# Expert weights in 2 MB transfers with 16 KB per partition, an eighth ring slot and four operand buffers

## The chip, the cores and the metric

One Trainium2 chip, one of its cores. The metric is the device time of one execution in microseconds, lower is better. The profile is one execution as the hardware profiler recorded it.

## What is computed

Three blocks in a row on 256 tokens of width 1024, all in fp32. The first is an attention and spatial-gating layer with a mixture of 16 experts, the second a macaron pair of half FFNs around an mLSTM mixer, the third an attention and an LRU layer. The change is in the experts of the first block:

```python
def expert_choice_ffn(h, w_router, w1, w3, w2):
    n, d = h.shape[1], h.shape[2]
    cap = CAPACITY_FACTOR * n // N_EXPERTS          # 32 tokens
    aff = jax.nn.softmax((h @ w_router).astype(jnp.float32), axis=-1)
    gate, idx = lax.top_k(jnp.swapaxes(aff, 1, 2), cap)
    xe = jax.vmap(lambda hb, ib: hb[ib])(h, idx)
    hid = jax.nn.silu(jnp.einsum('becd,edf->becf', xe, w1)) * jnp.einsum('becd,edf->becf', xe, w3)
    ye = jnp.einsum('becf,efd->becd', hid, w2) * gate[..., None].astype(h.dtype)
```

Each of the 16 experts has w1 and w3 of 1024 x 2048 and w2 of 2048 x 1024, 8 MB each in fp32: 384 MB in all, each byte read once and used for 32 tokens.

## The kernel before

Five programs, one for each engine, are written out by hand, in order, and meet through semaphores. Each engine has one semaphore on which it counts its instructions; `at(name)` is the count at which a named step is done. All loads of weights are issued by SP.

**The ring.** Weights go through `ring`, `NSLOT` = 7 slots of 1 MB (2048 fp32 in each of 128 partitions). `Ring.place` (L96) gives each load the next slot in turn, and passes over slots that are held. `load` (L220) has SP wait until the former owner of the slot is released, `("free", name)`, and issues the DMA. SP works strictly in order, so a load whose slot is not free holds up all that follow. `sp_experts` (L1681) issues for each expert x eight loads `(w1,x,kk)` of 128 rows, eight `(w3,x,kk)`, and eight `(w2,x,c,hf)` of 256 rows, each 1 MB with 8 KB in one run per partition. A slot `gs` is held during expert 0 for the scatter weights, with no load.

**The experts on TensorE.** `pe_experts` (L1715) waits for each load and multiplies it with the gathered tokens: w1 and w3 at L1775, w2 at L1799, four products side by side on 32 columns each. The last product that reads a slot releases it. Between w3 and w2 stands the turn of the expert: VectorE multiplies (L1945), TensorE transposes `sil` (L1789), VectorE copies the result (L1947, `hid`), and w2 begins. After w2 VectorE scales `ye` (L1956), and TensorE scatters it during the next expert (L1759).

**The second block's units.** A part of the second block is woven into the experts as 44 units, from expert 2 on, one in about 7.5 of the 24 places of an expert (`unit_at`). Unit u brings one load, a chunk `(s,12+u)` of 1 MB, mostly with 1 KB rows; two units bring none, and after unit 34 the number is one less. ScalarE (L323) and VectorE (L329) split a chunk into a high and a low part in `WB`; the end of VectorE's split releases the slot. On VectorE the units stand at fixed places in the order: those of the w1 places at the beginning of the expert, those of the w3 places before its product, those of the w2 places after `hid`. TensorE multiplies the chunk a unit later (L231 to L233).

**The operands.** The down projections (`pe_rows`, L457) of the later blocks use activations that ScalarE (`act_operand`, L492) and VectorE (`dve_operand`, L499) split into `RB`, two buffers; operand n waits until TensorE has finished with operand n-2. `pe_rows` holds back operand nk-2 and works off the last two together.

Of the kernel before, what the change touches and what calls it, by code (L numbers as in the profile page):

```python
# [11 lines left out]
D = 1024  # L12
NSLOT = 7
BIG = 12626
# [70 lines left out]
class Ring:  # L85
# [7 lines left out]
    def clear(self):  # L93
        self.i, self.owner, self.count, self.held = 0, [None] * NSLOT, [0] * NSLOT, {}

    def place(self, name, hold, loads):  # L96
        while self.i % NSLOT in self.held.values():
            self.i += 1
        i = self.i % NSLOT
        self.i += 1  # L100
        before, self.owner[i] = self.owner[i], name
        self.count[i] += 16 * loads
        self.slot[name], self.value[name], self.before[name] = i, self.count[i], before
        if hold:
            self.held[name] = i
        return i, before

# [34 lines left out]
def _build(nc, I, out, ctx):  # L142
# [10 lines left out]
    WB = sb("WB", [128, 2, 2, 2048], F32R)  # L153
    RB = sb("RB", [128, 2, 2, 512], F32R)
    big = sb("big", [128, BIG])
# [64 lines left out]
    def load(sp, name, src, n, pat=None, hold=False, parts=128, **dims):  # L220
        i, before = R.place(name, hold, 1)
        if before is not None:
            sp.wait_ge(*at("free", before))
        sp.dma_start(slot(name, n, pat, parts, **dims), src).then_inc(R.sem[i], 16)

    def free_before(name):
# [10 lines left out]

    def rows2(w, c0=0, n=D):  # L240
# [58 lines left out]
    def load_chunk(sp, c):  # L299
        src, n, pat, dims = CH[c]  # L300
        if not isinstance(src, tuple):
            load(sp, ("s", c), src, n, pat, **dims)
            return
        i, before = R.place(("s", c), False, 2)
        sp.wait_ge(*at("free", before))
        for q in range(2):
            sp.dma_start(slot(("s", c), n, pat, **dims)[:, q], src[q]).then_inc(R.sem[i], 16)
# [80 lines left out]

    def pe_turning(pe, name, tiles, regions, xn, waits=(), ends=(), b0=0):
        for w in waits:  # L390
            pe.wait_ge(*at(*w))
        for kk in range(8):
            b = b0 + kk % 4
            if kk >= 4:
                pe.wait_ge(*at("turned", name, kk - 4, 0))
                if len(regions) == 2:
                    pe.wait_ge(*at("turned", name, kk - 4, 1))
            for i, (ap, n, r, c) in enumerate(tiles):
                z = 0 if c < regions[0][1] else 1
                if kk == 0:  # L400
                    pe.wait_ge(*at("xn", name, i))
                closes = i + 1 == len(tiles) or (z == 0 and len(regions) == 2 and tiles[i + 1][3] >= regions[0][1])
                e = pe.transpose(PB[4 * z + b][:, c:c + n], xn(i)[0:n, kk * 128:kk * 128 + 128], ident[0:n, 0:n])
# [116 lines left out]

    def act_row(act, name, dst, bank):
        for z in range(2):
            yield
            act.wait_ge(*at("row", name, z))
            act.activation(dst[:, 512 * z:512 * z + 512], PB[bank][:, :], ACT.Copy).then_inc(*A(("rowed", name, z)))

# [216 lines left out]
    def pe_gemv(pe, group, waits):  # L743
        def pick(v):
            pe.wait_ge(*at("mraw", v))
            raw, rows_ = gemv_raw(v), ident.rearrange("p (j c) -> p j c", j=4)[:, :, 0:2]
            for i in range(4):
                if v == TWO:
                    for a in range(2):
                        e = pe.matmul(gemv_bank(v)[:, 8 * i:8 * i + 4].rearrange("p (j c) -> p j c", c=2), raw[:, 128 * i:128 * i + 128],  # L750
                                      rows_[:, 2 * a:2 * a + 2], start=a == 0, stop=a == 1)
                else:
                    e = pe.matmul(gemv_bank(v)[:, 8 * i:8 * i + 8].rearrange("p (j c) -> p j c", c=2), raw[:, 128 * i:128 * i + 128],
                                  rows_, start=True, stop=True)
            e.then_inc(*P(("pick", v)))
# [303 lines left out]
    def act_first(act):  # L1059
# [54 lines left out]
        for n in range(4):  # L1114
            steps(g2, 2)
        run(act_row(act, "gt", gt1, 5))

# [563 lines left out]
    def sp_experts(sp, g2):  # L1681
        steps(g2, 8)
        load(sp, "router", I["w_router"][0].rearrange("(a p) n -> p a n", p=128), 128, "p (a n) -> p a n", a=8)
        run(g2)
# [30 lines left out]
    def pe_experts(pe, g2):  # L1715
# [9 lines left out]
        steps(g2, 8)  # L1725
        pe_turn(pe, "h2", TL2, REG_2, lambda i: xn_2[:, i, :], between=route)
        pe.wait_ge(*at("aff"))
# [10 lines left out]
        for kk in range(8):  # L1738
# [3 lines left out]
            for i in range(2):  # L1742
                pe.matmul(PB[b][:, :], xh[:, i, kk * 128:kk * 128 + 128], posr[:, i, :], start=i == 0, stop=False)
                e = pe.matmul(PB[b][:, :], xl[:, i, kk * 128:kk * 128 + 128], posr[:, i, :], start=False, stop=i == 1)
            e.then_inc(*P(("gathered", kk)))
# [20 lines left out]
        for x in range(16):  # L1766
            for half, name in ((0, "w1"), (1, "w3")):
                if x:
                    pe.wait_ge(*at("ye", x - 1, half))
                for kk in range(8):  # L1770
                    steps(ctx_units, len(units(x, 8 * half + kk)))
                    s = slot((name, x, kk))
                    pe.wait_ge(*landed((name, x, kk)))
                    for j in range(4):
                        e = pe.matmul(PB[half][32 * j:32 * j + 32, :], xeT[:, kk, 32 * x:32 * x + 32], s[:, 512 * j:512 * j + 512],  # L1775
                                      start=kk == 0, stop=kk == 7)
                    e.then_inc(*P(("free", (name, x, kk)), *([("up", x, half)] if kk == 7 else [])))
                    if x and half == 0 and kk % 2:
# [8 lines left out]
            for j in range(4):  # L1787
                c0 = 256 * (j // 2) + j % 2
                e = pe.transpose(PB[0][:, 128 * j:128 * j + 128], sil[:, c0:c0 + 255:2], ident)  # L1789
            e.then_inc(*P(("hid_turned", x)))  # L1790
            pe.wait_ge(*at("hid", x))
            for c in range(4):
                steps(ctx_units, len(units(x, 16 + 2 * c, 2)))
                for n in range(2):
                    for j in range(4):
                        if n == 0 and j % 2 == 0:
                            pe.wait_ge(*landed(("w2", x, c, j // 2)))
                        s = slot(("w2", x, c, j // 2), 2048, "p (j n) -> p j n", j=2)
                        e = pe.matmul(PB[n][32 * j:32 * j + 32, :], hidT[:, j, 32 * c:32 * c + 32],  # L1799
                                      s[:, j % 2, 512 * n:512 * n + 512], start=c == 0, stop=c == 3)  # L1800
                        if n == 1 and j % 2:
                            e.then_inc(*P(("free", ("w2", x, c, j // 2)), *([("down", x)] if c == 3 and j == 3 else [])))
            if x == 1:
# [5 lines left out]
    def act_experts(act, sp_, g2):  # L1809
# [24 lines left out]
        for x in range(16):  # L1834
# [8 lines left out]
            if x == 0:  # L1843
                scatter_weights(1)
                run(act_row(act, "gt2", gt2, 4))
            steps(ctx_units, len(units(x, 16, 8)))
# [1778 lines left out]
def layout(I):  # L3625

    def c(v):
        v = np.asarray(v).reshape(-1)
        return v.reshape(-1, 128).T
    b_in = np.asarray(I["b_in_2"])[0]  # L3630
# [4 lines left out]
    parts = {"c": c(I["c"]), "c_ctx": c(I["c_ctx"]), "b_mod": c(I["b_mod"]), "g_mix": c(I["g_mix"]),  # L3635
             "g_ffn": c(I["g_ffn"]), "c_2": c(I["c_2"]), "c_ctx_2": c(I["c_ctx_2"]), "b_ada_2": c(I["b_ada_2"]),
             "norm_g_2": c(I["norm_g_2"]), "b_q": c(b_in[512:1536]), "b_k": c(b_in[1536:2560]),
# [34 lines left out]
```

## Time and profile before

| | before |
|---|---|
| time, median of 3 runs | 2356.17 us (2351.1 to 2356.51) |
| span of the profiled execution | 2347.7 us |
| TensorE busy (matmul) | 1993.4 us, 85% |
| VectorE / ScalarE busy | 962.5 us, 41% / 734.3 us, 31% |
| moved by DMA | 672.10 MB, mean 286 GB/s |
| mean granted TensorE clock | 0.935 of 2.4 GHz |

The span runs from the first to the last instruction; the time of an execution also has what lies around it, 8.5 us more in the median. The page's slices are 58.7 us each. The experts stand from 270 to 1350 us, the first block's attention before them, the second and third blocks after them.

### The profile page before, as it was taken

How to read it: one execution, taken by the hardware profiler on the slowest of the kernel's cores; microseconds unless marked ns; L12 is line 12 of the kernel's file. 1: busy time of each engine (PE TensorE's matmuls, PEld its weight loads, DVE VectorE, ACT ScalarE, POOL GpSimd, SP SyncE). 2: the span in 40 equal slices, each digit the busy share in tenths (PEclk: the TensorE clock that was granted, in tenths of full speed). 3: DMA queues.
4: the chain of work that ended last, by engine and by line, in shares of the span. 5: the costliest groups of instructions: out<-in, count | busy, mean ns of one | idle time of the engine just before them, and what ended most of it. 6: DMA issues, size and time to landing. Idle time of an engine off the chain costs nothing.

```text
span 2347.7 us, 29615 instructions
## 1 busy us (share of the span) xinstructions
PE 1993.4 (85%) x12486; PEld 1349.9 (57%) x12486; DVE 962.5 (41%) x1623; ACT 734.3 (31%) x1190; POOL 42.6 (2%) x47
## 2 busy tenths in 40 slices
PE   6999767778777777777778789989999899999997
PEld 3656313333334333333434389968999899785686
DVE  3534321122122122212434254567664645653486
ACT  4322221011111111112211054454654544543365
POOL 0000000000000000000000000000000000000010
PEclk8989899898999899898889999999999999999999
DMA  9967899999999999999999965535444455350430
GB/s 371 418 244 273 330 409 418 413 413 414 414 417 411 412 414 416 413 410 406 410 396 413 412 209 183 173 112 161 126 142 164 162 171 187 110 186 19 144 131 23
DMA packets 210436, 672.10 MB, mean 286 GB/s; under 512 B 11504, under 2 KB 134512, under 8 KB 152192
## 3 DMA queue, kind: packets, MB, share of 16 engines
q1 hardware_dynamic: 210304, 670.21, 74.3%
q8 instruction: 99, 1.62, 0.3%
q14 instruction: 33, 0.27, 0.0%
HBM read 669.12 MB, written 1.05 MB: 285 GB/s over the span
## 4 chain that ended last, share of the span: by engine, by line
PE 54%; DMA 30%; DVE 11%; ACT 3%; issue 2%; SPq 0%; POOL 0%; DVEq 0%; ACTq 0%
DMA ring<-in_w 22%; PE pb L231 12%; PE pb L233 12%; PE pb L232 12%; DMA ring<-in_w_a 5%; PE pb L1775 3%; DVE WB L329 3%; PE pb L1799 2%; DMA ring<-in_w_in 2%; PE pb L770 2%; ACT WB L323 1%; DMA ring<-in_w_mod 1%; PE pb L994 1%; PE pb L964 1%; PE pb L3053 1%
## 5 line engine op out<-in xcount | busy, mean ns | idle before, releaser
L329 DVE TENSOR_TENSOR WB<-ring,WB 128x1024 fp32r<-128x1024 f32 (+3 forms) x370 | 426.4, 1194 | 454.1 <-ACT WB L323 453.4
L323 ACT ACTIVATE WB<-ring 128x1024 fp32r<-128x1024 f32 (+3 forms) x370 | 361.3, 1025 | 725.9 <-DMA ring<-in_w_a 456.8
L231 PE MATMUL pb<-HH,WB 128*128 128x256 f32 (+1 forms) x1680 | 494.1, 294 | 11.1 <-DVE WB L329 4.3
L232 PE MATMUL pb<-HL,WB 128*128 128x256 f32 (+1 forms) x1680 | 483.6, 288 | 0.0
L233 PE MATMUL pb<-HH,WB 128*128 128x256 f32 (+1 forms) x1680 | 483.3, 288 | 0.0
L1775 PE MATMUL pb<-ring,big 128*32 128x512 f32 x2048 | 296.3, 671 | 149.5 <-DMA ring<-in_w 132.5
L231 PEld LDWEIGHTS pb<-HH,WB 128*128 128x128 f32 x1680 | 330.4, 197 | 38.3 <-issue 23.2
L232 PEld LDWEIGHTS pb<-HL,WB 128*128 128x128 f32 x1680 | 330.5, 197 | 2.2 <-issue 2.1
L233 PEld LDWEIGHTS pb<-HH,WB 128*128 128x128 f32 x1680 | 329.9, 196 | 0.0
L1775 PEld LDWEIGHTS pb<-ring,big 128*32 128x32 f32 x2048 | 47.4, 113 | 362.1 <-DMA ring<-in_w 274.8
L1799 PE MATMUL pb<-ring,big 128*32 128x512 f32 x1024 | 166.6, 644 | 55.5 <-DMA ring<-in_w 46.9
L231 PE MATMUL pb<-WB,RB 128*128 128x512 f32 x376 | 154.1, 410 | 11.8 <-DVE RB L501 11.0
L232 PE MATMUL pb<-WB,RB 128*128 128x512 f32 x376 | 150.4, 400 | 0.0
L233 PE MATMUL pb<-WB,RB 128*128 128x512 f32 x376 | 150.0, 399 | 0.0
L1799 PEld LDWEIGHTS pb<-ring,big 128*32 128x32 f32 x1024 | 35.5, 113 | 164.6 <-DMA ring<-in_w 99.5
L231 PE MATMUL pb<-WB,HH 128*128 128x256 f32 (+2 forms) x368 | 120.9, 328 | 7.8 <-DVE big L2750 2.8
L233 PE MATMUL pb<-WB,HL 128*128 128x256 f32 (+2 forms) x368 | 118.2, 321 | 0.0
L232 PE MATMUL pb<-WB,HH 128*128 128x256 f32 (+2 forms) x368 | 118.0, 321 | 0.0
L1926 DVE TENSOR_TENSOR X<-X,pb 128x512 f32<-128x512 f32 x64 | 44.0, 687 | 163.7 <-PE pb L1759 163.5
L231 PEld LDWEIGHTS pb<-WB,RB 128*128 128x128 f32 x376 | 73.1, 194 | 39.3 <-DVE RB L501 14.0
L1759 PE MATMUL pb<-big 128*128 128x512 f32 x128 | 72.9, 656 | 17.0 <-DVE X L1926 16.2
L770 PE MATMUL pb<-ring,cs 128*32 128x512 f32 x480 | 66.7, 681 | 20.0 <-DMA ring<-in_w_mod 18.1
(450 smaller groups left out, 1955.3 us busy)
## 6 DMA issues: line engine op xcount, KB each, us to landing
ring<-in_w SPq DMA_DIRECT2D x384, 1024.0 KB, 14.3
ring<-in_w_a SPq DMA_DIRECT2D x66, 1024.0 KB, 11.8
ring<-in_w_in SPq DMA_DIRECT2D x38, 1024.0 KB, 7.0
ring<-in_w_ada SPq DMA_DIRECT2D x36, 1024.0 KB, 6.6
ring<-in_w_b SPq DMA_DIRECT2D x33, 1024.0 KB, 5.0
ring<-in_w_mod SPq DMA_DIRECT2D x24, 1024.0 KB, 11.1
ring<-in_w_out SPq DMA_DIRECT2D x8, 1024.0 KB, 6.1
ring<-in_b_w_in SPq DMA_DIRECT2D x8, 1024.0 KB, 6.5
```

The costliest lines, as they stand in the source:

```text
L231: pe.matmul(o, l[0], r[0], start=start, stop=False)
L232: pe.matmul(o, l[0], r[1], start=False, stop=False)
L233: return pe.matmul(o, l[1], r[0], start=False, stop=stop)
L323: act.activation(WB[:, c % 2, 0, x:y], flat[:, x:y], ACT.Copy).then_inc(*A(("high", c, z)))
L329: dve.tensor_tensor(WB[:, c % 2, 1, x:y], flat[:, x:y], WB[:, c % 2, 0, x:y].bitcast(F32), ALU.subtract).then_inc(*V(("low", c, z), *([("f ...
L770: e = pe.matmul(gemv_bank(v)[32 * j:32 * j + 32, :], cs_flat[:, 16 * which + 2 * kk:16 * which + 2 * kk + 32], s[:, 512 * j:512 * j + 512] ...
L964: pe.matmul(PB[3 + n % 3][:, :], qT1[r:r + 64, pl, 128 * i:128 * i + 128], kT1[r:r + 64, :], start=True, stop=True).then_inc(*P(("scores1" ...
L994: e = pe.matmul(PB[2 * (h % 2) + z][:, 256 * s_:256 * s_ + 256], kT1[r:r + 64, c:c + 128], qT1[r:r + 64, pl, :], start=True, stop=True)
L1759: pe.matmul(PB[moe_bank(x, i, j)][:, :], gT[:, x, 128 * i:128 * i + 128], ye[:, 512 * j:512 * j + 512], start=True, stop=True).then_inc(*P ...
L1775: e = pe.matmul(PB[half][32 * j:32 * j + 32, :], xeT[:, kk, 32 * x:32 * x + 32], s[:, 512 * j:512 * j + 512], start=kk == 0, stop=kk == 7)
L1799: e = pe.matmul(PB[n][32 * j:32 * j + 32, :], hidT[:, j, 32 * c:32 * c + 32], s[:, j % 2, 512 * n:512 * n + 512], start=c == 0, stop=c == 3)
L1926: dve.tensor_tensor(y, y, PB[moe_bank(x, i, j)][:, :], ALU.add).then_inc(*V(("moe", x, i, j)))
```

## The change

- `ring` has 8 slots. Each expert matrix is loaded in four transfers of 2 MB, each into two neighbouring slots (`place_pair`), with 16 KB in one run per partition: `(w1,x,q)`, `(w3,x,q)` with q = 0 to 3, `(w2,x,c)` with c = 0 to 3. A transfer is released when both its halves have been used.
- `place_pair` takes the pointer's slot and the next. Where the next is beyond slot 7 or one of the two is held, it puts the slot into a list `left` (if it isn't itself held) and moves on. `place` for a single load that is not held takes the last entry of `left` first.
- A pair of rows of w1 lies in one partition, so the model width is used in another column order (`by_pairs`) by the transposes of `xn_2`, the gather of the tokens, the columns of modulation, bias and gain, and the router. `act_row` brings two gate rows back into the usual order. w2 has four rows in a partition, so `sil` is transposed in steps of four columns.
- The loads of the units stand ahead of the pair whose places they share.
- `RB` has four buffers; operand n waits for operand n-4.
- The scratch space of the DMA rings is reduced, which makes room.

The core of the diff:

```diff
-NSLOT = 7
+NSLOT = 8
+    def take(self, i, n, name, loads):
+        before = [x for x in dict.fromkeys(self.owner[i:i + n]) if x is not None]
+        self.owner[i:i + n] = [name] * n
+        self.count[i] += 16 * loads
+        self.slot[name], self.value[name] = i, self.count[i]
+        self.before[name] = before[0] if before else None
+        return i, before
+
     def place(self, name, hold, loads):
+        if self.left and not hold:
+            return self.take(self.left.pop(), 1, name, loads)
         while self.i % NSLOT in self.held.values():
             self.i += 1
         i = self.i % NSLOT
         self.i += 1
...
+    def place_pair(self, name):
+        while True:
+            i = self.i % NSLOT
+            held = [j for j in (i, i + 1) if j in self.held.values()]
+            if i + 1 < NSLOT and not held:
+                break
+            if i not in held:
+                self.left.append(i)
+            self.i += 1
+        self.i += 2
+        return self.take(i, 2, name, 1)
...
+    def load_pair(sp, name, src):
+        i, before = R.place_pair(name)
+        for b in before:
+            sp.wait_ge(*at("free", b))
+        sp.dma_start(pair(name), src).then_inc(R.sem[i], 16)
...
+    def by_pairs(kk):
+        c = 256 * (kk // 2) + kk % 2
+        return slice(c, c + 255, 2)
...
     def rb(n, w):
-        return RB[:, n % 2, 0, 0:w], RB[:, n % 2, 1, 0:w]
+        return RB[:, n % 4, 0, 0:w], RB[:, n % 4, 1, 0:w]
...
-        if n >= 2:
-            act.wait_ge(*at("operand", name, n - 2))
+        if n >= 4:
+            act.wait_ge(*at("operand", name, n - 4))
...
             for name, w_ in (("w1", w1), ("w3", w3)):
-                for kk in range(8):
-                    for u in units(x, 8 * (name == "w3") + kk):
+                for q in range(4):
+                    for u in units(x, 8 * (name == "w3") + 2 * q, 2):
                         load_unit(u)
-                    load(sp, (name, x, kk), w_[x, kk * 128:kk * 128 + 128, :], 2048)
+                    load_pair(sp, (name, x, q), w_[x, 256 * q:256 * q + 256, :].rearrange("(p b) n -> p (b n)", b=2))
...
             for c in range(4):
-                for hf in range(2):
-                    for u in units(x, 16 + 2 * c + hf):
-                        load_unit(u)
-                    load(sp, ("w2", x, c, hf), w2[x, 512 * c + 256 * hf:512 * c + 256 * hf + 256, :].rearrange("(p b) n -> p (b n)", b=2), 2048)
+                for u in units(x, 16 + 2 * c, 2):
+                    load_unit(u)
+                load_pair(sp, ("w2", x, c), w2[x, 512 * c:512 * c + 512, :].rearrange("(p b) n -> p (b n)", b=4))
...
                 for kk in range(8):
                     steps(ctx_units, len(units(x, 8 * half + kk)))
-                    s = slot((name, x, kk))
-                    pe.wait_ge(*landed((name, x, kk)))
+                    s = pair((name, x, kk // 2))
+                    if kk % 2 == 0:
+                        pe.wait_ge(*landed((name, x, kk // 2)))
...
-                e = pe.transpose(PB[0][:, 128 * j:128 * j + 128], sil[:, c0:c0 + 255:2], ident)
+                e = pe.transpose(PB[0][:, 128 * j:128 * j + 128], sil[:, j:j + 509:4], ident)
```

## Rows read from the trace of the kernel before

**Rows 1.** The page, part 2: tenths in 40 slices of 58.7 us.

```profile
PE   6999767778777777777778789989999899999997
...
DMA  9967899999999999999999965535444455350430
GB/s 371 418 244 273 330 409 418 413 413 414 414 417 411 412 414 416 413 410 406 410 396 413 412 209 183 173 112 161 126 142 164 162 171 187 110 186 19 144 131 23
```

**Rows 2.** Busy time by stretch: us, engines busy, clock, DMA share, GB/s.

```profile
core 0: us, PE busy (x) PEld busy (x) DVE busy (x) ACT busy (x) POOL busy (x), PEclk, DMA share, GB/s
308.00:368.00 60.00, 39.73 (x225) 8.49 (x219) 13.85 (x27) 8.20 (x16) 0.00 (x0) 0.91 1.01 421
270.00:1346.00 1076.00, 828.31 (x5132) 376.35 (x5124) 265.74 (x408) 150.50 (x210) 4.96 (x4) 0.91 1.01 411
1408.00:1467.00 59.00, 59.00 (x494) 59.00 (x493) 29.04 (x34) 24.27 (x31) 0.00 (x0) 1.00 0.57 186
```

**Rows 3.** The chain of waits, 270 to 1346 us, shares by line.

```profile
by line: DMA ring<-in_w 47.2%; DMA ring<-in_w_a 11.2%; PE pb L1775 7.1%; PE pb L1799 5.0%; PE pb L231 4.8%; PE pb L232 4.4%; PE pb L233 4.4%; DMA ring<-in_w_in 3.9%; DVE WB L329 2.8%; ACT WB L323 1.3%; PE pb L1759 1.3%; issue 0.7%; DVE tmpT
```

**Rows 4.** Loads issued from L224, 308 to 368 us.

```profile
L224 SPq DMA_DIRECT2D ring<-in_w x26: 327/328/679, 308.2 to 367.5; - x26
...
DMA to landing us min/median/max: 12.5/15.4/16.2
```

**Rows 5.** The same, 127 to 170 us, where the queue runs empty.

```profile
L224 SPq DMA_DIRECT2D ring<-in_w_ada x10: 327/328/328, 127.2 to 169.3; - x10
...
DMA to landing us min/median/max: 4.8/5.3/6.7
```

**Rows 6.** Timeline of expert 6: start, duration, what, idle before; w3, turn, chunk.

```profile
700.43 1.94 PE L1775 MATMUL pb<-ring,big 128*32 128x512 f32 x8 [1.42 <-DMA ring<-in_w]
...
702.92 1.94 PE L1775 MATMUL pb<-ring,big 128*32 128x512 f32 x8 [0.55 <-DMA ring<-in_w]
...
705.41 1.70 PE L1775 MATMUL pb<-ring,big 128*32 128x512 f32 x8 [0.55 <-DMA ring<-in_w]
707.19 0.69 DVE L1945 TENSOR_TENSOR big<-big,pb 128x512 f32<-128x512 f32 x1 [13.26 <-PE pb L1775]
...
708.71 0.69 DVE L1947 COPY big<-pb 128x512 f32<-128x512 f32 x1 [0.84 <-PE pb L1789]
710.89 2.00 ACT L323 ACTIVATE WB<-ring 128x1024 fp32r<-128x1024 f32 x2 [18.41 <-DMA ring<-in_w_a]
```

**Rows 7.** Timeline at the start of expert 0.

```profile
270.64 38.59 SPq L224 DMA_DIRECT2D ring<-in_w  x19
...
276.23 1.06 PE L1775 MATMUL pb<-ring,big 128*32 128x512 f32 x8 [1.34 <-DMA ring<-in_w]
```

**Rows 8.** Timeline, the split of a chunk in expert 8.

```profile
863.56 2.01 ACT L323 ACTIVATE WB<-ring 128x1024 fp32r<-128x1024 f32 x2 [16.87 <-DMA ring<-in_w_a]
...
864.65 2.36 DVE L329 TENSOR_TENSOR WB<-ring,WB 128x1024 fp32r<-128x1024 f32 x2 [14.46 <-ACT WB L323]
```

**Rows 9.** Timeline at the last operand of the first half FFN.

```profile
1547.45 0.42 ACT L497 ACTIVATE RB<-big 128x256 fp32r<-128x256 f32 x1 [2.30 <-PE pb L233]
...
1547.90 0.43 DVE L501 TENSOR_TENSOR RB<-big,RB 128x256 fp32r<-128x256 f32 x1 [1.79 <-ACT RB L497]
...
1548.47 0.47 PE L231 MATMUL pb<-WB,RB 128*128 128x512 f32 x1 [1.12 <-DVE RB L501]
```

**Rows 10.** TensorE's waits, 1350 to 2348 us: total, times, longest.

```profile
PE pb L231 <- DVE RB L501: 11.0, 8, 3.2
```

**Rows 11.** Groups of instructions by line: busy, mean ns, idle before.

```profile
L582 PEld LDWEIGHTS pb<-K,big 128*128 128x128 f32 x80 | 14.7, 212 | 25.8 <-DVE big L623 25.8
...
L1789 PEld LDWEIGHTS pb<-K,big 128*128 128x128 f32 x64 | 9.6, 209 | 34.8 <-DVE big L1945 34.5 <-issue 0.2
...
L525 ACT ACTIVATE big<-pb 128x512 f32<-128x512 f32 x6 | 3.6, 597 | 11.2 <-PE pb L519 11.2
```

More of the change, by code:

```diff
@@ L100, in place @@
         self.i += 1
-        before, self.owner[i] = self.owner[i], name
-        self.count[i] += 16 * loads
-        self.slot[name], self.value[name], self.before[name] = i, self.count[i], before
         if hold:
             self.held[name] = i
-        return i, before
+        return self.take(i, 1, name, loads)
+    def place_pair(self, name):
[9 more added lines that the diff above has]
+        return self.take(i, 2, name, 1)
     def let_go(self, name):
@@ L221, in load, with pair @@
         i, before = R.place(name, hold, 1)
-        if before is not None:
-            sp.wait_ge(*at("free", before))
+        for b in before:
+            sp.wait_ge(*at("free", b))
         sp.dma_start(slot(name, n, pat, parts, **dims), src).then_inc(R.sem[i], 16)
+    def pair(name):
+        i = R.slot.get(name, 0)
+        return ring[:, i:i + 2, :].rearrange("p s n -> p (s n)")
+    def load_pair(sp, name, src):
+        i, before = R.place_pair(name)
+        for b in before:
+            sp.wait_ge(*at("free", b))
+        sp.dma_start(pair(name), src).then_inc(R.sem[i], 16)
     def free_before(name):
@@ L304, in load_chunk @@
         i, before = R.place(("s", c), False, 2)
-        sp.wait_ge(*at("free", before))
+        for b in before:
+            sp.wait_ge(*at("free", b))
         for q in range(2):
@@ L384, in act_scaled, with pe_turning @@
                 act.activation(xn(i)[0:n, :], ap, ACT.Copy, scale=st[0:n, r:r + 1]).then_inc(*A(("xn", name, i)))
-    def pe_turning(pe, name, tiles, regions, xn, waits=(), ends=(), b0=0):
+    def pe_turning(pe, name, tiles, regions, xn, waits=(), ends=(), b0=0, block=by_blocks):
         for w in waits:
@@ L1115, in act_first @@
             steps(g2, 2)
-        run(act_row(act, "gt", gt1, 5))
+        run(act_row(act, "gt", gt1, 5, True))
         for q in (0, 2):
@@ L1682, in sp_experts @@
         steps(g2, 8)
-        load(sp, "router", I["w_router"][0].rearrange("(a p) n -> p a n", p=128), 128, "p (a n) -> p a n", a=8)
+        load(sp, "router", I["w_router"][0].rearrange("(q p b) n -> p q (b n)", q=4, b=2), 128, "p (q n) -> p q n", q=4)
         run(g2)
@@ L1725, in pe_experts @@
         steps(g2, 8)
-        pe_turn(pe, "h2", TL2, REG_2, lambda i: xn_2[:, i, :], between=route)
+        pe_turn(pe, "h2", TL2, REG_2, lambda i: xn_2[:, i, :], between=route, block=by_pairs)
         pe.wait_ge(*at("aff"))
@@ L1795, in pe_experts @@
                     for j in range(4):
-                        if n == 0 and j % 2 == 0:
-                            pe.wait_ge(*landed(("w2", x, c, j // 2)))
-                        s = slot(("w2", x, c, j // 2), 2048, "p (j n) -> p j n", j=2)
+                        if n + j == 0:
+                            pe.wait_ge(*landed(("w2", x, c)))
+                        s = pair(("w2", x, c)).rearrange("p (j n) -> p j n", j=4)
                         e = pe.matmul(PB[n][32 * j:32 * j + 32, :], hidT[:, j, 32 * c:32 * c + 32],
-                                      s[:, j % 2, 512 * n:512 * n + 512], start=c == 0, stop=c == 3)
-                        if n == 1 and j % 2:
-                            e.then_inc(*P(("free", ("w2", x, c, j // 2)), *([("down", x)] if c == 3 and j == 3 else [])))
+                                      s[:, j, 512 * n:512 * n + 512], start=c == 0, stop=c == 3)
+                e.then_inc(*P(("free", ("w2", x, c)), *([("down", x)] if c == 3 else [])))
             if x == 1:
@@ L1844, in act_experts @@
                 scatter_weights(1)
-                run(act_row(act, "gt2", gt2, 4))
+                run(act_row(act, "gt2", gt2, 4, True))
             steps(ctx_units, len(units(x, 16, 8)))
```

39 lines of the change are left out of this document (24 added, 15 removed).

## The prediction

> **What bounds the kernel now.** I read the page's forty slices first: from slice 6 to slice 23 the DMA row stands at 9, GB/s at 390 to 418, while TensorE stands at 6 to 8 [rows 1]. The table by stretch gives the same stage in one row: 270 to 1346 us, 1076 us, the 16 DMA engines at a share of 1.01 and 411 GB/s, TensorE busy 828 us [rows 2]. The chain of waits over that stretch is 62% DMA into `ring` (47.2 + 11.2 + 3.9) [rows 3]. So in 46% of the span the DMA queue is the bound, and a microsecond in which it has nothing to move is a microsecond of the kernel. What keeps it full is depth: a 1 MB load there lands 12.5 to 16.2 us after its issue [rows 4], the time of some six loads, while a load into an empty queue needs 4.8 [rows 5]. After 1350 us DMA is at about half (0.57) and TensorE has no gap in a whole slice [rows 2]: there the change can act only through the operand buffers.
>
> Two prices follow. Successive expert loads let TensorE start at 700.43, 702.92 and 705.41: 2.49 us for 1 MB [rows 6]. So an empty queue costs 4.8 - 2.49 = 2.3 us between an issue and full flow. Call it the restart.
>
> **Part 1, longer runs.** The cost of a packet by its length: at 1 KB rows 186 GB/s at share 0.57 is 326 GB/s for busy engines, 50.2 ns for each 1,024-byte packet on one of 16; at 8 KB rows 421 at 1.01 is 417, 314.4 ns [rows 2]. The slope is 264.2 / 7168 = 0.0369 ns a byte, the constant 12.5 ns. A 16 KB packet is then 616.5 ns instead of 628.8, 2.0%. The 1 KB rows come from a queue with pauses, which inflates their price, so I take 1.7%, with 0 (long rows are cut again) and 3% as bounds. The 192 pairs cost 2 x 2.49 = 4.98 us each now; 192 x 4.98 x 0.017 = 16 us saved (0 to 28). The Trainium skill, page "DMA: Bandwidth & Descriptors", section "Bandwidth", gives a fixed 3 cycles a packet, 3.5 ns at its 850 MHz, where the rows give 12.5; by it, as an estimate, the gain would be 5 us. Its ceiling of 435 GB/s would leave 3% above the 421 of the trace.
>
> **Part 2, where the loads go.** This part decides. I walked `Ring.place` and `place_pair` through the load order of `sp_experts` and noted for each load whose release SP awaits and how many MB were issued behind that one. Before: always 6 (5 while `gs` is held). After: mostly 7 or 5, but not always, because of `left`. `place_pair` puts a slot that it skips into `left`, the pointer laps and a later pair takes that slot in the ordinary way, yet it stays in `left`, and the next chunk of the second block takes it, whoever has it by then. Three kinds result.
>
> (a) A chunk is put into the slot of the pair issued just before: `(s,30)` behind `(w1,7,3)`, `(s,46)` behind `(w3,12,3)`, `(s,48)` behind `(w1,13,2)`. SP waits until that pair has landed and been multiplied; nothing is queued behind. TensorE takes 1.06 us for 1 MB [rows 7], 2.1 for a pair (3.9 at the lower clock of [rows 6], 1.94 each). Idle: 2.1 + 2.3 = 4.4 us, three times, 13.2.
>
> (b) A pair needs slots 6 and 7 just after a chunk went to 7: `(w1,6,1)` behind `(s,26)`, `(w1,11,1)` behind `(s,42)`. SP waits for the split of the chunk. ScalarE starts at 863.56, VectorE ends at 864.65 + 2.36 = 867.01: 3.45 us [rows 8]. Idle: 3.45 + 2.3 = 5.75, twice, 11.5.
>
> (c) The same at the turn of an expert: `(w2,6,0)` behind `(s,28)`, `(w2,11,0)` behind `(s,44)`. The split stands on VectorE behind `hid`, which needs the last w3. From that landing: 2.1 for TensorE, then 2.3 from the end of its matmuls (707.11) to the end of the copy (709.40), then 2.36 of VectorE; 6.8. The chunk lands 3.0 after w3 (710.89 - 705.41 - 2.49) [rows 6, 8]. Idle: 6.8 - 3.0 + 2.3 = 6.1, twice, 12.2.
>
> (d) Seven pairs wait for a chunk with one pair (4.9 us) between: `(w1,2,1)`, `(w3,2,1)`, `(w2,4,3)`, `(w3,5,2)`, `(w2,9,3)`, `(w3,10,2)`, `(w1,15,3)`. Idle: 5.75 - 4.9 = 0.9 each, 6.
>
> (e) In expert 0 `gs` has slot 3, slot 2 can't be paired, and only three pairs circulate, 6 MB as before but released two at a time. Before, SP resumes at 270.64, 1.1 us after TensorE's start [rows 7]; then 2.1. With the pauses for the scatter weights, where the released pair again comes late: 3 us (1 to 5).
>
> (f) 54 pairs cover halves of two former pairs and have 5 MB behind the later one, 12.4 us. A pair takes 2.1, a unit of the second block on TensorE between them about 6, a turn 2.3, the restart 2.3: 12.7. So it is about even where a unit and a turn meet, and short where the heavier units of experts 10 to 14 stand. No row prices that; bounds 0 and 20 us, I take 6, near the lower end since few of the 44 units meet a turn.
>
> Sum of idle: 13.2 + 11.5 + 12.2 + 6 + 3 + 6 = 52 us. All of it falls on the bound; nothing later in the stage can win it back, since the share is 1.01 [rows 2].
>
> **Part 3, four operand buffers.** `act_operand` of the last operand waits for the last but two; `pe_rows` holds its last two operands back, so TensorE meets an unready operand at the end of each down projection: ScalarE 1547.45, VectorE 1547.90, TensorE 1548.47 after 1.12 us idle [rows 9]. Of the 11.0 us in eight waits [rows 10] five are of this kind, in fa, wo2, fb, wo3 and wob; 5 x 1.12 = 5.6 us go (4 to 6). The other three wait for VectorE's states and stay. Next after it is the split of the chunk, which has landed and been split earlier.
>
> **Part 4, the rest.** The eighth slot before 270 us: the queue is full there only from about 60 to 120 us, by rate [rows 1]; elsewhere TensorE and VectorE set the pace. 1 us gained (0 to 3). Strided reads of the weights for transposes: the `sil` transposes already read every second column, at 209 ns a weight load against 212 for unstrided ones [rows 11]; stride 4 isn't shown, 64 loads, bounds 0 and +0.2 us each, 13 at most but under the waits for DMA, so 0. Six copies with interleaved columns, 0.6 us each [rows 11], up to twice that; 0 (to 3). The router's load has half as many pieces and lands before it is needed; 0. After the last load TensorE works 2 us as before; 0.
>
> **The sum.** -16 + 52 - 5.6 - 1 = +29.4 us. The profiled span is 2347.7; the median of the three runs is 2356.2, 8.5 more, which I leave as it is: 2377 for a span, **2386** for the time.
>
> **The rivals.** *Free transfers (faster).* The releases come early enough or the waits of (a) to (c) lie where the queue has slack; then 2356 - 16 - 5.6 - 1 = 2333. For it: TensorE idles a quarter of the stage. Against it: the share of 1.01, and in (a) to (c) nothing is queued at all. It decides if the idle adds up to less than 16 us. 0.10. *Even.* Idle between 16 and 30 us, 2356. 0.06. *Cascade.* In (f) every one of the 44 units leaves the ring 1.5 us short: 66 instead of 6, 2446. For it: 12.4 against 12.7 above. Against it: most units stand away from turns. 0.09. *Rows cut again.* The 16 KB runs move in packets as before, part 1 is 0: 2402. 0.10. *A fixed price per transfer.* If each transfer paid its restart in a full queue, 192 fewer would save 192 x 2.3 = 442 us, 1914. The 2.49 us between successive starts [rows 6] against 4.8 [rows 5] speak against that. 0.01. The fit in the same page of the Trainium skill, section "Anatomy of one DMA", has such a fixed 2.0 us per DMA and its rule is to batch; the trace shows it hidden in a full queue. *The forecast* has 0.64.
>
> **Range.** Low: (a) to (c) 37, (d) to (f) 6, gain 22 + 7: +14, 2370; a little below it to take in part of the even case, 2367. High: (f) 20, lower clock in (a) and (c) 9 more, gain 8: 37 + 9 + 6 + 3 + 20 - 8 - 5 = +62, cut to 2414, since they hardly all meet. The measurement tells 0.3%, 7 us, from no change. Faster: free transfers and the fixed price, 0.11. Same: 0.06. Slower: forecast, cascade and cut rows, 0.83.
>
> **What would show it.** Right: GB/s near 428 where several pairs run in a row; holes of 4 to 6 us in the DMA row at seven places of the stage, with SP waiting for TensorE's or VectorE's release; no waits of 1.12 us at the ends of the down projections; the stage ending some 36 us later. Wrong: a share of 1.01 through the stage (then the free transfers hold), or idle of a microsecond or two at every unit (cascade). The prediction fails most easily on (f) and on the 1.7%.

## The result, and the profile after

| | before | after |
|---|---|---|
| time, median | 2354.22 us (2351.1 to 2356.51) | 2439.45 us (2438.82 to 2440.01) |
| span of the profiled execution | 2347.7 us | 2438.6 us |
| mean granted TensorE clock | 0.935 | 0.909 |

The change makes the kernel slower: ratio 1.0371, 95% interval 1.0354 to 1.0387, 85 us. The forecast was 2386 us, 2367 to 2414. The sign was right, the size was not. (The median of before now has a fourth run in it.)

The page of after, part 2, the last two rows as in [rows 1]; a slice is 61.0 us:

```profile
DMA  9967798999997999998979995534517445351330
GB/s 385 414 241 290 304 417 356 421 386 378 403 370 306 423 394 392 389 371 358 379 310 373 370 379 185 179 108 163 159 62 233 157 158 188 122 179 52 123 128 18
```

The flat 410 to 418 GB/s of [rows 1] has gone. Two slices, 421 and 423, are above everything that before shows; next to them stand 356, 306 and 310. The long runs are faster, and the queue is stopped more. The stretches of after, in the columns of [rows 2]:

```profile
270.00:1440.00 1170.00, 834.67 (x5133) 397.83 (x5136) 266.26 (x411) 150.33 (x210) 4.96 (x4) 0.86 0.93 378
...
540.00:730.00 190.00, 137.12 (x840) 66.38 (x840) 36.64 (x45) 21.19 (x27) 0.00 (x0) 0.88 0.94 386
```

The expert stage ends at 1440 us, not at 1346; its DMA share is 0.93 for 1.01. TensorE is busy 834.7 us in it, for 828.3: its work is nearly the same, it waits more. The chain of waits of the stage begins, in the form of [rows 3]:

```profile
by line: DMA ring<-in_w 51.5%; PE pb L1816 10.1%; DMA ring<-in_w_a 7.8%; PE pb L260 4.1%; PE pb L1840 3.9%; PE pb L261 3.7%; PE pb L262 3.6%; DVE WB L366 2.7%; DMA ring<-in_w_in 1.9%; PE pb L1798 1.2%; PE pb L1522 1.1%; issue 1.0%; SPq L253
```

L1816, the product with w1 and w3 (L1775 of before), has risen from 7.1% to 10.1% of a longer stretch: where the queue is empty, the chain goes from a transfer to the products that read it, to their release, and to the next transfer.

**The queue's time, load by load.** For each load of the stage I took the distance between its landing and the one before, and subtracted what the load takes in a full queue: 2.487 us for 1 MB in 8 KB runs, 4.898 us for a pair in 16 KB runs, 2.5 to 2.97 us for a chunk. What is left is called idle time of the queue. In every kernel it also holds about 4 us in which the queue isn't idle but moves two loads that don't go to the ring, `b_v` ahead of `(s,48)` (1.4 us) and `ctx_2` ahead of `(w2,3,0)` (2.5 us); they cancel in differences. The count begins behind the first 6 MB of the experts. The two kernels, and the twelve that follow, compare so. Idle and end of stage are from the profiled execution, whose own time can lie off the median of the runs: it was 2377.5 us in e1, 2352.7 in e3, 2354.5 in e4, 2346.8 in e12. Each ratio is against before on the same chip; before had medians of 2349 to 2353 us there:

| kernel | time, us | ratio to before, 95% | last w2 landed, us | idle of the queue, us |
|---|---|---|---|---|
| before | 2354.2 | | 1346.7 | 24.2 |
| after | 2439.5 | 1.0371 (1.0354 to 1.0387) | 1439.9 | 130.3 |
| e1_no_left | 2385.0 | 1.0138 (1.0114 to 1.0161) | 1379.5 | 72.9 |
| e2_short_runs | 2448.2 | 1.0402 (1.0381 to 1.0423) | 1444.3 | 124.0 |
| e3_rb4 | 2347.3 | 0.9971 (0.9958 to 0.9985) | 1351.3 | 26.1 |
| e4_8slots | 2349.6 | 0.9988 (0.9977 to 0.9998) | 1345.5 | 23.2 |
| e5_halves | 2357.7 | 1.0014 (1.0000 to 1.0029) | 1352.3 | 44.7 |
| e6_left_halves | 2418.8 | 1.0276 (1.0252 to 1.0301) | 1416.4 | 110.3 |
| e7_8slots_rb4 | 2343.6 | 0.9961 (0.9948 to 0.9974) | 1339.5 | 21.7 |
| e8_wrap | 2346.7 | 0.9960 (0.9945 to 0.9975) | 1344.5 | 33.2 |
| e9_wrap_units_first | 2333.2 | 0.9921 (0.9903 to 0.9939) | 1330.7 | 21.3 |
| e10_units_first | 2400.5 | 1.0214 (1.0195 to 1.0233) | 1397.3 | 88.8 |
| e11_no_left_first | 2346.8 | 0.9969 (0.9955 to 0.9983) | 1344.4 | 35.2 |
| e12_halves_first | 2340.7 | 0.9936 (0.9918 to 0.9954) | 1344.9 | 36.1 |

After against before: 14.3 us less for moving the bytes (1044.1 for 1058.4), 106.1 us more idle, the last w2 93.2 us later, and 2.4 us less for all that follows it. So the loss is idle time of the queue in the expert stage; the question is which waits make it.

**Who stops the queue.** SP's own waits in the stage of after, 270 to 1440 us: total, times, longest. A wait of SP is harmless while enough is queued behind it; these are only the candidates.

```profile
SPq L252 <- PE pb L1816: 205.5, 42, 17.5
SPq L252 <- DVE WB L366: 194.3, 17, 23.1
```

By kind of the prediction the idle of after is: (a) 6.8, 5.8, 4.6 at the three chunks, 17.2 (the third, `(s,48)`, lands 8.88 us behind the pair, but it takes 4.3 in the kernels where the queue does not stop there, 2.9 for itself and 1.4 for `b_v`); (b) 6.5 and 6.8, 13.2; (c) 9.4 and 8.5, 17.9; (d) 16.4 at seven pairs; (e) 1.8; and what remains above the 24.2 us of before, the kind (f), 39.6, most of it at pairs whose last release is 4 or 5 MB back. A replay of the placement gives 83 pairs with 5 MB and 21 with 4 MB behind the release that they await. Six of the 21 belong to expert 0; the other 15 wait for a slot that a chunk had, and lose 21 us, the 83 lose 23. Two of the stops of kind (f) are `(w3,13,3)` with 8.9 us and `(w3,14,1)` with 5.5.

One stop of kind (a) and one of kind (f), in the timeline of after (columns as in [rows 6]). First the chunk `(s,30)`, issued from L243:

```profile
788.19 1.92 PE L1816 MATMUL pb<-ring,big 128*32 128x512 f32 x16
...
790.18 0.38 SPq L243 DMA_DIRECT2D ring<-in_w_a  x1
```

The pair ahead of it was multiplied until 790.11, and 0.07 us later SP issues the chunk. Nothing is queued, as forecast. But the queue had run empty at 785.5 us already (the chunk lands at 795.3, 9.75 us behind the pair): TensorE, late from a unit two pairs before, took the landed pair up only at 788.19. Then `(w3,8,2)`, issued from L253:

```profile
864.07 1.93 PE L1816 MATMUL pb<-ring,big 128*32 128x512 f32 x8 [4.87 <-DMA ring<-in_w]
865.93 0.29 PEld L260 LDWEIGHTS pb<-WB,RB 128*128 128x128 f32 x1 [1.66 <-issue]
...
872.47 0.39 PE L262 MATMUL pb<-WB,RB 128*128 128x512 f32 x1
...
872.78 1.06 PE L1816 MATMUL pb<-ring,big 128*32 128x512 f32 x8
...
873.96 0.33 SPq L253 DMA_DIRECT2D ring<-in_w  x1
```

TensorE is idle for 4.87 us until `(w1,8,3)` has landed whole. Then it multiplies the first half, then works off a unit of the second block, 865.93 to 872.86, then multiplies the second half and releases. SP issues `(w3,8,2)` at 873.96; the queue's last transfer had landed at 873.79. This is the place where most of what I missed lies.

### The profile page after: what moved, and what is told of

Same layout as the page of the kernel before. It is cut to its first block, busy times and chain, and to the rows that moved or that the text cites. A ratio compares the mean times of both kernels' runs of the same rounds, so it can differ in the third digit from the quotient of the medians.

```text
span 2438.6 us, 29505 instructions
## 1 busy us (share of the span) xinstructions
PE 2002.8 (82%) x12486; PEld 1376.0 (56%) x12486; DVE 958.7 (39%) x1623; ACT 731.6 (30%) x1190; POOL 42.6 (2%) x47
## 4 chain that ended last, share of the span: by engine, by line
PE 53%; DMA 30%; DVE 10%; ACT 3%; issue 2%; SPq 1%; POOL 0%; DVEq 0%; ACTq 0%; POOLq 0%
DMA ring<-in_w 25%; PE pb L260 12%; PE pb L261 11%; PE pb L262 11%; PE pb L1816 5%; DMA ring<-in_w_a 4%; DVE WB L366 3%; PE pb L1840 2%; PE pb L810 2%; ACT WB L360 1%; DMA ring<-in_w_mod 1%; DMA ring<-in_w_in 1%; PE pb L1034 1%; PE pb L1798 1%; PE pb L1004 1%
## 5 line engine op out<-in xcount | busy, mean ns | idle before, releaser
L1816 PE MATMUL pb<-ring,big 128*32 128x512 f32 x2048 | 299.8, 710 | 202.1 <-DMA ring<-in_w 196.7
L260 PEld LDWEIGHTS pb<-HH,WB 128*128 128x128 f32 x1680 | 334.6, 199 | 43.7 <-issue 27.1
L262 PEld LDWEIGHTS pb<-HH,WB 128*128 128x128 f32 x1680 | 334.1, 199 | 0.0
L1816 PEld LDWEIGHTS pb<-ring,big 128*32 128x32 f32 x2048 | 60.2, 119 | 394.9 <-DMA ring<-in_w 217.6
L1840 PE MATMUL pb<-ring,big 128*32 128x512 f32 x1024 | 153.1, 730 | 85.2 <-DMA ring<-in_w 79.0
L1840 PEld LDWEIGHTS pb<-ring,big 128*32 128x32 f32 x1024 | 30.9, 121 | 179.6 <-DMA ring<-in_w 108.9
L260 PEld LDWEIGHTS pb<-WB,RB 128*128 128x128 f32 x376 | 73.8, 196 | 34.6 <-issue 11.5
## 6 DMA issues: line engine op xcount, KB each, us to landing
ring<-in_w SPq DMA_DIRECT2D x192, 2048.0 KB, 14.3
```

Source lines behind the costliest of these rows:

```text
L260: pe.matmul(o, l[0], r[0], start=start, stop=False)
L262: return pe.matmul(o, l[1], r[0], start=False, stop=stop)
```

## The experiments

**e1 to e4: one part each.** e1 leaves the list of skipped slots unused, so that every load goes on round the ring; a skipped slot is lost for that lap.

```diff
-            if i not in held:
-                self.left.append(i)
```

> The changed kernel with one edit: a slot that place_pair skips is not put into left, so single loads take the pointer's slot. By a replay of the placement every load then has at least 4 MB queued behind the load whose release it awaits; the seven distances of 0 and the seven of 2 are gone. Theory placement (stale entries of left make the loss): the seven holes with nothing queued (49.7 us in the trace of the changed kernel) and the seven with one pair queued (16.4 us) go, and so does most of the other 39 us, time 2335 to 2350. Rival coarse release (2 MB are released at once, and 5 MB behind are too few at a unit): only those 66 us go and some 40 remain, 2365 to 2385. Rival transfer size (2 MB transfers in themselves are slow): above 2420.

Measured 2385.0 us, 54.5 less than after and at the upper end of the rival of the coarse release. Kinds (a) to (d) are gone (0.8 us is left of them), and 49 us of idle above before are still there, so the stale slots are half of the loss and not its whole.

e2 gives each pair as two transfers of 1 MB, 8 KB in one run, same slots, waits and releases.

```diff
-        sp.dma_start(pair(name), src).then_inc(R.sem[i], 16)
+        for h in range(2):
+            sp.dma_start(pair(name)[:, 2048 * h:2048 * h + 2048], src[:, 2048 * h:2048 * h + 2048]).then_inc(R.sem[i], 16)
```

> The changed kernel with each 2 MB transfer issued as two of 1 MB with 8 KB runs, into the same slots, with the same waits and the same release. It isolates the length of the runs. By the prediction's part 1 and the 4.90 us between landings of successive pairs (twice 2.49 before) it costs 0.08 us a pair, 15 us: 2454. If long runs are worth nothing: 2439. If 2 MB transfers hurt: below 2435.

Measured 2448.2, 8.7 more than after, where 15 were expected: 13.8 us more for moving the bytes, 6.3 less idle. In moving, the long runs are worth what was forecast; in time, less. Whether they go out whole is also in the count of packets, part 3 of the page, first before, then after:

```profile
q1 hardware_dynamic: 210304, 670.21, 74.3%
```

```profile
q1 hardware_dynamic: 182144, 670.20, 71.0%
```

28,160 fewer packets for the same bytes. The 192 pairs halved from 256 to 128 packets are 24,576 of them. Another 3,072 are packets of 4 bytes, of which the traces show 16 for each transfer, and there are 192 transfers fewer; the last 512 are missing in e2 too, whose count is 209,792. Rows are not cut again.

e3 and e4 are before with four operand buffers, and before with eight slots.

```diff
-    RB = sb("RB", [128, 2, 2, 512], F32R)
+    RB = sb("RB", [128, 4, 2, 512], F32R)
...
-NSLOT = 7
+NSLOT = 8
```

> The kernel before with four operand buffers and nothing else. By part 3 of the prediction five waits of 1.12 us at the ends of the down projections go: 5.6 us faster than before, 2348.6. Rival: the wait moves to the split of the last chunk, 0 to 2 us.

> The kernel before with eight slots of 1 MB, and nothing else but the smaller scratch space. By part 4 of the prediction about 1 us faster (0 to 3), 2353. Rival: depth is short at the heavier units of experts 12 to 14 (landings 1 to 1.4 us late there) and at the start of expert 0, then 4 to 8 us faster.

e3: 0.9971, 6.8 us less than before on the same chip, 3.5 to 9.9 by the interval, and 4.7 by the medians (2347.3 and 2352.0). TensorE's waits behind the stage in e3, the row that answers to [rows 10] (11.0 us in eight waits):

```profile
PE pb L231 <- DVE RB L501: 6.5, 4, 3.4
```

After has 5.6 us in three waits there. The five waits of 1.12 us are gone or nearly so. e4: 0.9988, 2.8 us (0.5 to 5.4), 2.4 by the medians. Both small terms hold in time.

**e5 and e6: release by halves.** The products of a pair give back each 1 MB slot when they have read it; e5 does it on top of e1, e6 on after with its list.

```diff
-        self.owner[i:i + n] = [name] * n
+        self.owner[i:i + n] = [name] if n == 1 else [(name, 0), (name, 1)]
...
-                    if kk % 2:
-                        e.then_inc(*P(("free", (name, x, kk // 2)), *([("up", x, half)] if kk == 7 else [])))
+                    e.then_inc(*P(("free", ((name, x, kk // 2), kk % 2)), *([("up", x, half)] if kk == 7 else [])))
```

> The changed kernel with passed-over slots forgotten (as in e1_no_left) and, besides, each 1 MB half of a pair handed back by TensorE as soon as it has read that half (four matmuls earlier than the other half for w1 and w3). Counting the ring's order out, the last release that a load of the expert stage needs then lies at most 4 MB back in 6 pairs, 5 MB in 114, 6 MB in 71; in e1_no_left it is 30, 126 and 35; in the kernel before it is 6 MB nearly everywhere. THEORY (what is left over the kernel before is the release of 2 MB at once: the ring has less work queued behind it, and the loss sits in the loads with the shortest distance): most of e1's 49 us of extra idle goes, total 2345 to 2368 us. RIVAL A (the loss is the 2 MB transfer itself, the 2.9 us of restart in place of 2.3 us and a longer wait at each stop): 2375 to 2385 us, as e1_no_left. RIVAL B (the lower TensorE clock costs it): also near 2380 us, with the granted clock of the stage unchanged against e1_no_left.

> The changed kernel as it is, passed-over slots kept in its list, and each 1 MB half of a pair handed back separately. Last release at 4 MB or less: 23 pairs (32 in the changed kernel), at 5 MB 37 (83), at 6 MB or more 132 (77). THEORY (two causes that add: stale slots cost 54 us, coarse release some 20 to 40 us): 2400 to 2422 us, that is, the coarse release is worth about the same with the list as without it. RIVAL (the two losses overlap, since a stop for one refills the slack for the other): 2425 to 2439 us. If the list only hurt because the release was coarse: 2350 to 2370 us.

e5: 2357.7, 27.3 less than e1; e6: 2418.8, 20.7 less than after. By the ratios, which take before on the same chip, it is 29 and 22 us. Both lie where the theory put them, and the list costs 61 us with halves, 54.5 without: two causes that add. Rival B falls too: the granted clock of 270 to 1340 us is 0.87 in e5 and 0.88 in e1, with 27 us between them. But e5 left one stop of 12.2 us at `(w3,13,3)`, which halves could not shorten; e8 showed why.

**e7 and e8: is it the 2 MB, or the ring?** e7 is before with both small parts and nothing else. e8 is e5 with no slot ever skipped: a pair takes the next two slots, and where these are not neighbours (22 of 192) it goes as two transfers with a wait each.

```diff
+        a, b = ab
+        if b == a + 1:
+            i, before = self.take(a, 2, name, 1)
+            self.both[name] = None
+            return ab, before
```

> The kernel before with 1 MB transfers of 8 KB runs, plus only the eighth slot and the four operand buffers. THEORY (the two are separate: 5.6 us and 1 us forecast, 4.7 to 6.8 and 2.4 to 2.8 us measured alone): 2343 to 2348 us, ratio to before 0.995 to 0.998. RIVAL (both cover the same stops): 2346 to 2350 us.

> As e5_halves, but a pair takes the next two slots of the ring whatever they are: neighbours get one transfer of 2 MB in 16 KB runs, slots 7 and 0 (22 pairs of 192) get two transfers of 1 MB in 8 KB runs, each with its own wait. No slot is ever passed over. Last release at 5 MB: 5 pairs, at 6 MB or more all others, as in the kernel before. THEORY (distance to the last release sets the idle time): the extra idle over the kernel before falls to 0 to 8 us, the long runs keep 0.077 us on 170 pairs, 13 us, the operand buffers 5 us: 2332 to 2345 us, which beats both kernels. RIVAL (a 2 MB transfer stops the queue more whatever the distance): 2355 to 2375 us.

e7: 2343.6, as forecast, faster than before. e8: 2346.7, between theory and rival. Its last releases are as far back as in before, yet it has 9 us more idle, nearly all of it in one stop: 10.05 us at `(w3,13,3)`, where before lost 1.9 about that place (3.3 with `b_v`). Its timeline:

```profile
1156.37 1.93 PE L1844 MATMUL pb<-ring,big 128*32 128x512 f32 x8 [6.18 <-DMA ring<-in_w]
1158.23 0.58 PE L289 MATMUL pb<-WB,HH 128*128 128x256 f32 x1
...
1165.77 1.07 PE L1844 MATMUL pb<-ring,big 128*32 128x512 f32 x8
...
1176.83 2.05 PE L1827 MATMUL pb<-big 128*128 128x512 f32 x2 [9.99 <-DVE X L1994]
```

and VectorE's longest wait between 1150 and 1190 us:

```profile
DVE big L1739 <- PE pb L291: 11.0, 1, 11.0
```

TensorE waits 6.18 us for a whole pair, multiplies one half, and only then does the unit (1158.23 to 1165.8) for which VectorE has waited 11.0 us, with ten more microseconds of VectorE's work behind it, for which TensorE in turn waits 9.99. The same unit and the same wait in before:

```profile
1161.88 0.39 PE L231 MATMUL pb<-WB,HH 128*128 128x256 f32 x1
...
1178.93 2.05 PE L1759 MATMUL pb<-big 128*128 128x512 f32 x2 [10.05 <-DVE X L1926]
```

The wait of ten microseconds is thus not new (10.05 in before, 9.13 in e9 below). What differs is when the unit begins: in before at 1161.88, when the first of the two MB had landed at 1160.38 and been multiplied, and 5.3 us ahead of the second at 1167.13; in e8 1.9 us behind the whole pair. That is the stop of the timeline at 864 us again, with a longer tail.

**e9 and e10: the unit ahead of the pair's wait.** One edit in the order on TensorE: the units of both halves are worked off before the wait for the pair. Their chunks are loaded ahead of the pair already. e9 is e8 with it, e10 is after with it.

```diff
-                    steps(ctx_units, len(units(x, 8 * half + kk)))
+                    if kk % 2 == 0:
+                        steps(ctx_units, len(units(x, 8 * half + kk, 2)))
```

> As e8_wrap, with one edit in TensorE's order: a context unit that stands at the odd half of a w1 or w3 pair is computed ahead of the wait for that pair, not between its two halves (its chunk is already loaded ahead of the pair). The trace of e8_wrap has one large stop left that the kernel before has not: 10.05 us ahead of w3,13,3, where 3.3 us are lost in before. There TensorE waited 6.2 us for the whole pair w1,13,3, landed at 1156.33, then computed one unit of 7 us until 1165.8, for which VectorE waited 11.0 us with a 21 us chain behind it; in before the unit started when the first MB had landed, while the second was still on its way. THEORY (waiting for 2 MB at once delays the unit that stands between the halves): the stop ahead of w3,13,3 falls to 2 to 5 us, the total to 2336 to 2343 us, ratio to before 0.992 to 0.996. RIVAL (the stop comes from the chain on VectorE alone, and the order on TensorE only moves the wait): 2344 to 2348 us, and the stop stays at 8 us or more.

> The changed kernel with only that edit in TensorE's order: units at an odd half ahead of their pair's wait. Its stop ahead of w3,13,3 is 8.94 us. THEORY: 5 to 8 us less there, 2 to 4 us at the other 14 units that stand at an odd half, total 2427 to 2434 us. RIVAL (the stale slots' and the coarse release's stops swallow it): 2435 to 2440 us.

e10: 2400.5, 39 us less than after, three to seven times what I expected. e9: 2333.2, 0.9921 (0.9903 to 0.9939), a little below the range in time and within it by ratio; it beats before and after, and e7 too (0.9948 to 0.9974). The stop at `(w3,13,3)` is 0.6 us in e9. The place of the timeline above, now in e10:

```profile
846.76 1.15 PE L260 MATMUL pb<-WB,RB 128*128 128x512 f32 x1
...
852.76 0.39 PE L262 MATMUL pb<-WB,RB 128*128 128x512 f32 x1
...
853.08 1.92 PE L1817 MATMUL pb<-ring,big 128*32 128x512 f32 x16
...
855.11 0.33 SPq L253 DMA_DIRECT2D ring<-in_w  x1
```

The unit runs from 846.76 to 853.15 while `(w1,8,3)` is on its way (landed 850.89), both halves follow without a gap, and `(w3,8,2)` is issued at 855.11, with the landing of 860.66 still ahead of it: no stop. My expectation counted the 15 units that stand at an odd half and one pair for each. An explanation, which no run takes apart, is that TensorE, once late by a unit, releases every pair late until the next wait for data, so that one unit costs at more than one pair. In e10 the idle at pairs with a last release 4 or 5 MB back is 18.8 us, of which 10.2 is the start of expert 0; in after it is 54.7, with 10.4. The 15 pairs with 4 MB lose 0.9 us in e10 for 21 in after, with the same placement: 4 MB behind the release is enough once the unit stands ahead of the wait.

**e11 and e12: the ladder.** e11 is after with the edits of e1 and e10, e12 adds the halves of e5.

> The changed kernel with two edits: passed-over slots forgotten (e1_no_left, 54 us alone) and units at an odd half ahead of their pair's wait (e10_units_first, 39 us alone). Releases stay those of 2 MB. THEORY (the two stops lie at different loads: the stale slots at 11 pairs and 3 chunks, the late units at the 104 pairs whose last release is 4 or 5 MB back, which fell from 54.7 to 18.8 us in e10): nearly additive, 2344 to 2354 us. RIVAL (without the list 156 pairs instead of 104 have a last release 4 or 5 MB back, and the coarse release stops them whatever stands between the halves): 2356 to 2370 us.

> As e11_no_left_first, and each half of a pair handed back by itself (e5_halves with TensorE's units first). In e5_halves 27 us came from the separate halves. THEORY (the units between the halves were what used the slack up, so the coarse release costs little once they are gone): 3 to 10 us less than e11, 2337 to 2347 us. RIVAL (the coarse release costs the same 20 to 27 us as in e5 and e6): 20 to 27 us less than e11. Against e9_wrap_units_first (2333.2 us) it shows what 42 passed-over slots are worth: 4 to 12 us more than that.

e11: 2346.8. From after the two edits take 92.7 us, alone they took 39.0 and 54.5: they add. e12: 2340.7, 6.1 us less, within the theory; the two intervals just miss each other. The profiled spans are alike (2345.1 and 2345.4), but that of e12 is the slowest of its four runs. The coarse release, 20 to 27 us while units stood between the halves, costs about 6 once they don't. From e12 to e9, with some 40 skipped slots less, it is 7.5 us by the medians but 3.5 by the ratios, whose intervals overlap, since before was 4 us slower beside e12 than beside e9; that term isn't clear of noise.

The ladder from after to e9, by medians and in brackets by ratios: unit ahead of the wait 39.0 (37), list 53.7 (58), halves 6.1 (8), no skipped slots 7.5 (3.5). What the change could have been shows in the GB/s of e9, slices of 58.3 us, beside [rows 1], and in a window of e9 and then of before:

```profile
GB/s 400 419 240 272 323 428 422 420 416 419 417 419 423 418 417 420 418 417 417 411 392 415 410 199 186 170 102 175 106 149 172 160 181 181 96 201 19 145 118 19
```

```profile
540.00:730.00 190.00, 143.24 (x918) 71.34 (x914) 38.38 (x46) 23.10 (x28) 0.00 (x0) 0.90 1.02 419
```

```profile
540.00:730.00 190.00, 149.76 (x927) 71.25 (x925) 38.96 (x47) 22.58 (x29) 0.00 (x0) 0.93 1.02 414
```

## Why the prediction was wrong

**Where the bound lies: right.** The loss is idle time of the DMA queue in the expert stage, and nearly nothing of it came back later: last w2 +93.2, profiled span +90.9. The medians differ by 85, since the profiled execution of before is a quick one.

**Longer runs, -16: right.** 14.3 us in the landings of after, 13.8 back again in e2. The 1.2% between 414 and 419 GB/s is a little less than the 1.5% of the landings, since e9 sends 22 pairs in short runs. The constant of a packet is thus nearer to 8 or 9 ns than to the 12.5 read off the 1 KB rows, where pauses inflate it, as the text allowed. This is an estimate: 14.3 us is 0.074 us a pair, in which each of the 16 engines moves 8 packets of data fewer and one of 4 bytes, so 74 / 9 = 8 ns if they cost alike, 74 / 8 = 9 if the small one is free. The 3.5 ns of the Trainium skill ("DMA: Bandwidth & Descriptors", section "Bandwidth") would, as an estimate, have given 5 us; the measurement decides.

**The placement, (a) to (d): right in place, short in size.** All 14 stops lie at the loads named. Measured against forecast: (a) 17.2 for 13.2, (b) 13.2 for 11.5, (c) 17.9 for 12.2, (d) 16.4 for 6; 64.7 for 43. The mis-sized parts are two. The restart was read from the quickest 1 MB load of [rows 5] (4.8 - 2.49 = 2.3; their median is 5.3); a pair into the empty queue lands 7.9 us after its issue at 873.96, so 7.9 - 4.9 = 3.0. That is 0.7 at each of 11 pairs, 8 us. And each term let TensorE start on a pair at its landing, when it was still behind with a unit: with the units out of the way, in e10, the chunks `(s,30)` and `(s,48)` lose 4.2 and 3.0 us, about the forecast 4.4 or less, in place of 6.8 and 4.6. The third chunk, `(s,46)`, loses 5.8 in both: it lands 6.7 us after its issue and not 5.1, and nothing shows why. The pairs of (b) to (d) did not shrink so in e10 (13.0, 17.4, 18.2). The larger restart explains (b) whole, and four of the seven pairs of (d) (1.5, 1.5, 1.8 and 0.7 where 0.9 + 0.7 would be due); what (c) and `(w1,2,1)` (5.8), `(w3,2,1)` (2.1) and `(w1,15,3)` (3.0) lose beyond it stays open.

**(e), start of the experts, 3: right**, 1.8.

**(f), 6: this step failed.** 39.6 us measured. The working had 12.7 us of work against 12.4 us of queued loads, with one unit of 6 in it, and called it even. It had 5 MB behind every release of this kind, where 15 pairs have only 4, 9.9 us of loads, so by its own sum they would have been 2.8 short where a unit and a turn meet. And it left out, which weighs more, that a pair is waited for as a whole: TensorE has nothing to do on the first half until the second MB has landed, 2.45 us later, and the unit, which used to fill just that time, comes after it. The unit's 6 us then stand between landing and release at each of the 15 pairs of w1 and w3 that have one between their halves. The diff shows it in two lines, the new wait at `kk % 2 == 0` and the unchanged `steps(ctx_units, ...)` of every kk above it; I costed the change's loads, waits and releases and not the step that stays where it was while the wait moves ahead of it. With the unit put back ahead of the wait the kinds (a) to (d) of e10 add to 61.7 and (e) to 1.6, and of its idle 88.8 - 61.7 - 1.6 - 24.2 = 1.3 us is left for (f). So 38 of the 39.6 us hang on that order. The coarse release is the other half of the cause, and not one in itself: with the order unchanged, halves handed back singly take 20.7 us off (e6); with the order mended they take about 6 (e12).

**Operand buffers, -5.6, and eighth slot, -1: right**, 5.4 by the waits of after (11.0 - 5.6) and 6.8 (3.5 to 9.9) by time; 2.8 (0.5 to 5.4) by time. In after itself the gain doesn't show in full: from the last w2 to the end it takes 2.4 us less than before. The 8.5 us that I put between span and time compared two executions: each run on record takes 1.2 to 1.5 us more than its own span, so the profiled execution of before, 2347.7, was simply quicker than its median, and before had medians of 2349 to 2353 in the later comparisons. That made the forecast 3 to 7 us high.

**The rivals.** Free transfers, even, rows cut again and a fixed price are out. The cascade rival, 2446 with 0.09, was the nearest in time and in what it says: units leave the ring short. But that its time came so near is partly luck. It had 66 us for (f) and none of the excess in (a) to (d). The argument against it, that most units stand away from turns, was beside the point, since it is not the turn that makes the unit late but the wait ahead of it. Lower clock: the clock did fall (0.91 to 0.85 over 270 to 1340 us), L1816 takes 710 ns a product for 671, but TensorE is busy hardly longer in the stage (834.7 us for 828.3), and between e1 and e5 the time moves by 27 us with the clock at 0.88 and 0.87. So it is not what sets the size of the loss.

## What to carry to other kernels

When a wait is merged, from one unit of data to two, look at everything that its engine does between the two old waits: it now stands behind the later one, and what hid in the time of the second transfer comes out on the path. Put such filler work ahead of the merged wait. And a slot that a ring sets aside has to be forgotten once the pointer takes it again; otherwise the next small load waits for the newest transfer, with nothing queued behind it.

## What the hardware showed that I had not expected

- A load of 2 MB into an empty queue mostly lands 7.7 to 8.1 us after its issue in after, 3.0 us more than in full flow. In e2, at the same places, two loads of 1 MB issued together mostly land within 7.4 to 7.8, 2.6 more. The 1 KB-row chunk at 790.18 has 2.1 (5.1 to landing, 2.97 in full flow), another, `(s,46)`, 3.9. So the price wasn't the same everywhere, and 2 MB in one transfer paid some 0.4 us more than in two.
- With stops in the queue the granted clock of the stage falls from 0.91 to 0.85 of 2.4 GHz (a mean over its levels of 1.2 and 2.4), while TensorE idles more; TensorE's time per product rises by 6% (671 to 710 ns). What that costs in later releases was not measured by itself.
- In the six kernels whose queue seldom stops (before, e3, e4, e7, e8, e9) the landings show a gap of 0.8 to 1.6 us in a full queue once in 206 to 215 us (e9: 526, 737, 944, 1158 us; before: 534, 742, 954). It is in the 24 us of before and nothing here explains it.
